# Output projection: the last two pairs of weight tiles taken chunk by chunk, and the norm's steps reordered to match

## The reference, cut to what matters

```
mix = jnp.concatenate([o.reshape(B, S, D_ATTN), rg], axis=-1) @ p['w_out'][l]
x = x + g2 * mix
h = _rmsnorm(x, ng[2]) * (1.0 + sc3) + sh3
x = x + g3 * 0.5 * _swiglu(h, p['ffn_w_gate'][l, 1], p['ffn_w_up'][l, 1], p['ffn_w_down'][l, 1])
```

## Time and profile before

| what | value |
|---|---|
| median of 3 runs | 2269.17 us |
| lowest, highest | 2267.47 us, 2271.68 us |
| time of the profiled execution | 2273.28 us |
| its span in the trace | 2271.5 us |
| PE busy in the span | 97% |
| DVE busy | 68% |
| ACT busy | 36% |
| output projection, pairs 1 to 3 on PE | about 1388.9 to 1465.3 us of the span |

### The profile page before, as it was taken

How to read it: one execution, slowest core, us unless ns; L and a number is a source line. 1 busy time by engine, 2 the same in 40 slices (tenths; PEclk the granted TensorE clock), 3 DMA queues, 4 the chain that set the end, 5 groups by cost and what they waited for, 6 DMA issues and landing times.

```text
span 2271.5 us, 33980 instructions
## 1 busy us (share of the span) xinstructions
PE 2196.6 (97%) x13144; PEld 2108.2 (93%) x13144; DVE 1552.8 (68%) x2607; ACT 816.1 (36%) x1458; POOL 20.2 (1%) x31
## 2 busy tenths in 40 slices
PE   5999999999999999999999999999999999999997
PEld 4989999999999999889977779899999999999996
DVE  6977677777888776666668874686455556756556
ACT  5632322334111143654255662453232323421122
POOL 0000000000000000000000030000000000000000
PEclk8999999999999999999989999999999999999998
DMA  7333333344524304010110011131212123431312
GB/s 290 132 105 133 104 124 113 107 135 134 202 93 158 126 21 156 19 47 29 32 49 22 22 40 38 56 114 60 86 58 87 58 87 101 157 122 52 107 43 84
DMA packets 82292, 210.10 MB, mean 92 GB/s; under 512 B 9856, under 2 KB 36352, under 8 KB 82176
## 3 DMA queue, kind: packets, MB, share of 16 engines
q1 hardware_dynamic: 82176, 208.52, 27.3%
HBM read 172.56 MB, written 35.92 MB: 92 GB/s over the span
## 4 chain that ended last, share of the span: by engine, by line
PE 89%; DVE 6%; DMA 2%; ACT 2%; issue 1%; SPq 1%; DVEq 0%; ACTq 0%
PE ps L717 15%; PE ps L718 15%; PE ps L719 15%; PE ps L792 9%; PE ps L794 9%; PE ps L793 9%; PE ps L972 6%; PE ps L1043 4%; PE ps L1072 2%; PE ps L1058 1%; PE ps L954 1%; DVE sb_nmx L2280 1%; DMA sb_stage<-in_w_mod 1%; DVE sb_hL L1752 1%; PE ps L741 1%
## 5 line engine op out<-in xcount | busy, mean ns | idle before, releaser
L717 PE MATMUL ps<-sb_hH,sb_wH 128*128 128x384 f32 x1664 | 563.1, 338 | 6.3 <-DVE sb_hL L1752 3.4
L718 PE MATMUL ps<-sb_hL,sb_wH 128*128 128x384 f32 x1664 | 557.8, 335 | 0.0
L719 PE MATMUL ps<-sb_hH,sb_wL 128*128 128x384 f32 x1664 | 557.6, 335 | 0.0
L717 PEld LDWEIGHTS ps<-sb_hH,sb_wH 128*128 128x128 f32 x1664 | 313.7, 189 | 13.1 <-DVE sb_hL L1752 4.6
L718 PEld LDWEIGHTS ps<-sb_hL,sb_wH 128*128 128x128 f32 x1664 | 313.7, 189 | 1.2 <-issue 0.3
L719 PEld LDWEIGHTS ps<-sb_hH,sb_wL 128*128 128x128 f32 x1664 | 313.8, 189 | 0.0
L2056 DVE SCALAR_TENSOR_TENSOR sb_x<-ps,sb_mod,sb_x 128x384 f32<-128x384 f32 (+2 forms) x384 | 186.3, 514 | 172.4 <-PE ps L719 167.0
L792 PE MATMUL ps<-sb_hH,sb_wH 128*128 128x384 f32 x704 | 235.4, 334 | 0.5 <-issue 0.3
L794 PE MATMUL ps<-sb_hH,sb_wL 128*128 128x384 f32 x704 | 235.2, 334 | 0.0
L793 PE MATMUL ps<-sb_hL,sb_wH 128*128 128x384 f32 x704 | 235.1, 334 | 0.0
L1226 ACT ACTIVATE sb_wH<-sb_wide 128x512 fp32r<-128x512 f32 x176 | 110.9, 632 | 228.0 <-DVE sb_wide L1806 222.9
(11 more groups left out here) (244 smaller groups left out, 3795.7 us busy)
## 6 DMA issues: line engine op xcount, KB each, us to landing
sb_raw<-in_w_gate SPq DMA_DIRECT2D x56, 512.0 KB, 3.6
sb_raw<-in_w_up SPq DMA_DIRECT2D x56, 512.0 KB, 3.6
sb_raw<-in_w_mod SPq DMA_DIRECT2D x56, 512.0 KB, 3.5
hidden<-sb_tmp SPq DMA_DIRECT2D x132, 192.0 KB, 2.2
sb_hid_raw<-hidden SPq DMA_DIRECT2D x40, 576.0 KB, 6.3
sb_raw<-in_w_dn SPq DMA_DIRECT2D x80, 256.0 KB, 2.6
sb_stage<-in_w_mod SPq DMA_DIRECT2D x4, 2048.0 KB, 15.7
sb_raw<-in_w_in SPq DMA_DIRECT2D x16, 512.0 KB, 3.5
```

The costliest lines, as they stand in the source:

```text
L717: pe.matmul(o, wH, xH, start=begin, stop=False)
L718: pe.matmul(o, wH, xL, start=False, stop=False)
L719: return pe.matmul(o, wL, xH, start=False, stop=end)
```

## The change

Pairs 0 and 1 stay as they are. The weights of pair 3 now go to `wjH` and `wjL`, so that pairs 2 and 3 are resident together, and PE takes these two pairs chunk by chunk: (2,0), (3,0), (2,1), (3,1), (2,2), (3,2). The helper `mix_nth` gives the place of a (pair, chunk, f) in the new order for the semaphore waits. `stats` and `spread` of chunks 0 and 1 move to new places in that order. The running sums of the norm move from `last_raw` to `o_first`. The orders of ACT and DVE are written anew: the `lo` of pair 3 now stands ahead of the nine sums, and the adds of pairs 2 and 3 follow chunk by chunk. The loops over `i` are written out.

```diff
-SQUARES[2] = [(c, k) for ks in (range(4), (4, 5), (6, 7)) for c in range(NC) for k in ks]
+SQUARES[2] = [(c, k) for ks in (range(4), range(4, KT)) for c in range(NC) for k in ks]
...
         def sum_buf(z, c):
 
+            if z == 2:
+                return o_first[:, c * CH:(c + 1) * CH]
             return tmp[:, 4] if z % 2 else last_raw[:, c * CH:(c + 1) * CH]
+
+        def mix_nth(i, c, f):
+
+            return i * 6 + 2 * c + f + 1 if i < 2 else 12 + 4 * c + 2 * (i - 2) + f + 1
...
             def out_chunk(i, c, between=None):
 
+                mH, mL = (wjH, wjL) if i == 3 else (wiH, wiL)
                 for f in range(2):
                     pe.wait_ge(raw_used[f], i + (used_wo[f] + 2))
-                    pe.wait_ge(w_x, i * 6 + (c * 2 + f + 1))
+                    if i:
+                        pe.wait_ge(w_x, 6 + mix_nth(i - 1, c, f))
                     for n, k in enumerate(MIX_ORDER):
-                        if isinstance(i, int) and i == 0:
+                        if i == 0:
                             pe.wait_ge(mix_lo, c * KT + n + 1)
-                        m = three(ps[:, f * NC + c, 0:CH], wiH[:, f, k * P:(k + 1) * P], wiL[:, f, k * P:(k + 1) * P],
+                        m = three(ps[:, f * NC + c, 0:CH], mH[:, f, k * P:(k + 1) * P], mL[:, f, k * P:(k + 1) * P],
...
-            with pe.Fori(0, 2) as i:
-                for c in range(NC):
-                    out_chunk(i + 1, c)
-            def last_chunks(at_stats, at_spread, c, before=None):
+            for c in range(NC):
+                out_chunk(1, c)
+            norm_at = {(2, 1, 8): (stats, 0), (3, 1, 2): (spread, 0), (2, 2, 8): (stats, 1), (3, 2, 8): (spread, 1)}
...
-            out_chunk(3, 0)
-            out_chunk(3, 1, last_chunks(12, None, 0))
-            out_chunk(3, 2, last_chunks(8, 3, 1, 0))
+            for c in range(NC):
+                for i in (2, 3):
+                    out_chunk(i, c, norm_steps(i, c))
             ffn_pe(1)
...
-            with act.Fori(0, 2) as i:
+            for i in range(2):
                 for f in range(2):
-                    cast(wiH[:, f], f, i + (used_wo[f] + 1), (w_ready, i * 6 + (5 + f)))
+                    cast(wiH[:, f], f, i + (used_wo[f] + 1), (w_ready, mix_nth(i, NC - 1, f)))
+            for f in range(2):
+                cast(wjH[:, f], f, 2 + (used_wo[f] + 1))
...
             load_root()
             for c in range(NC):
                 squares(2, c, x_mixed, range(4))
-            for f in range(2):
-                cast(wiH[:, f], f, 2 + (used_wo[f] + 1), (w_ready, 12 + (5 + f)))
+            squares(2, 0, x_mixed, (4, 5))
...
-            with dve.Fori(0, 2) as i:
-                w_adds(i)
+            for f in range(2):
+                lo(wjL[:, f], f, None, wjH[:, f], whi_wo + 7 + f)
             for c in range(NC):
                 for k in range(1, 4):
                     sum_square(2, c, k)
-            w_adds(2)
+            w_add(2, 0, 0)
+            w_add(2, 0, 1)
+            sum_square(2, 0, 4)
+            sum_square(2, 0, 5)
             early_low(1, 0, 0)
             early_low(1, 1, 0)
+            w_add(3, 0, 0)
+            sum_square(2, 0, 6)
             shift_step(1)
-            for c in range(NC):
-                for k in (4, 5):
-                    sum_square(2, c, k)
-            for f in range(2):
-                w_add(3, 0, f)
-            sum_square(2, 0, 6)
+            w_add(3, 0, 1)
             sum_square(2, 0, 7)
-            w_add(3, 1, 0)
+            w_add(2, 1, 0)
+            inverse_of(2, 0)
             early_low(1, 0, 1)
             early_low(1, 1, 1)
-            inverse_of(2, 0)
-            w_add(3, 1, 1)
-            sum_square(2, 1, 6)
-            sum_square(2, 1, 7)
+            w_add(2, 1, 1)
+            sum_square(2, 1, 4)
+            sum_square(2, 1, 5)
...
             def rest(k):
-                if k == 2:
-                    w_add(3, 2, 0)
+                if k == 1:
+                    w_add(3, 1, 0)
+                    sum_square(2, 1, 6)
                 elif k == 3:
-                    inverse_of(2, 1)
+                    w_add(3, 1, 1)
+                    sum_square(2, 1, 7)
                 elif k == 5:
-                    w_add(3, 2, 1)
-                elif k == 7:
-                    sum_square(2, 2, 6)
-                    sum_square(2, 2, 7)
+                    w_add(2, 2, 0)
+                    sum_square(2, 2, 4)
 
             apply(2, 0, rest)
+            inverse_of(2, 1)
+            w_add(2, 2, 1)
+            sum_square(2, 2, 5)
+            for k in (6, 7):
+                w_add(3, 2, k - 6)
+                sum_square(2, 2, k)
             inverse_of(2, 2)
             ffn_dve(1)
```

More of the change, by code:

```diff
@@ L1132, in _, with norm_steps @@
                 out_chunk(0, c, lambda n: outputs(*later[c, n]) if (c, n) in later else None)
-            with pe.Fori(0, 2) as i:
-                for c in range(NC):
-                    out_chunk(i + 1, c)
-            def last_chunks(at_stats, at_spread, c, before=None):
+            for c in range(NC):
+                out_chunk(1, c)
+            norm_at = {(2, 1, 8): (stats, 0), (3, 1, 2): (spread, 0), (2, 2, 8): (stats, 1), (3, 2, 8): (spread, 1)}
+            def norm_steps(i, c):
                 def between(n):
[L1138 to L1143, removed]
-                return between
-            out_chunk(3, 0)
-            out_chunk(3, 1, last_chunks(12, None, 0))
-            out_chunk(3, 2, last_chunks(8, 3, 1, 0))
+                    if (i, c, n) in norm_at:
+                        do, at = norm_at[i, c, n]
+                        do(2, at)
+                return between
+            for c in range(NC):
+                for i in (2, 3):
+                    out_chunk(i, c, norm_steps(i, c))
             ffn_pe(1)
@@ L1617, in _ @@
                     mix_high(c, k)
-            with act.Fori(0, 2) as i:
+            for i in range(2):
                 for f in range(2):
-                    cast(wiH[:, f], f, i + (used_wo[f] + 1), (w_ready, i * 6 + (5 + f)))
+                    cast(wiH[:, f], f, i + (used_wo[f] + 1), (w_ready, mix_nth(i, NC - 1, f)))
+            for f in range(2):
+                cast(wjH[:, f], f, 2 + (used_wo[f] + 1))
             def x_mixed(c, k):
-                return w_x, 6 + (12 if k < 4 else 18) + (2 * c + k - 5 if k > 5 else 0)
+                return w_x, 6 + mix_nth(k // 2, c, k % 2)
             load_root()
@@ L1632, in _ @@
             early_cast(1, 1, 0)
-            for c in range(NC):
-                squares(2, c, x_mixed, (4, 5))
             squares(2, 0, x_mixed, (6, 7))
+            root_of(2, 0)
             early_cast(1, 0, 1)
             early_cast(1, 1, 1)
-            root_of(2, 0)
-            squares(2, 1, x_mixed, (6,))
+            squares(2, 1, x_mixed, (4, 5))
             root_copy(2, 0)
-            squares(2, 1, x_mixed, (7,))
             for k in range(KT):
                 h_hi(2, 0, (k,))
-                if k == 2:
-                    squares(2, 2, x_mixed, (6,))
+                if k == 1:
+                    squares(2, 1, x_mixed, (6,))
                 elif k == 3:
+                    squares(2, 1, x_mixed, (7,))
+                elif k == 5:
                     root_of(2, 1)
-                elif k == 5:
-                    squares(2, 2, x_mixed, (7,))
+                    squares(2, 2, x_mixed, (4,))
+            squares(2, 2, x_mixed, (5,))
             root_copy(2, 1)
+            squares(2, 2, x_mixed, (6, 7))
             root_of(2, 2)
@@ L2355, in w_add @@
             def w_add(i, c, f):
-                dve.wait_ge(w_ready, i * 6 + (2 * c + f + 1))
+                dve.wait_ge(w_ready, mix_nth(i, c, f))
                 for cond, b, e in conds(c):
@@ L2364, in _ @@
             dve.wait_ge(xback, 16 * KT)
-            def w_adds(i):
+            for i in range(2):
                 for c in range(NC):
```

## The result

The changed kernel takes 2275.74 us (median of 10 runs, 2274.62 to 2278.00), the kernel before 2269.64 us (10 runs, 2267.47 to 2274.52). The ratio is 1.0028, with a 95% interval of 1.0019 to 1.0036: slower by 6.1 us, 4.3 to 8.2. The prediction was +5.9 us, 2275.1 us.

What follows compares the result with a forecast made beforehand. PE, busy 97% of the span, was taken to bound the kernel. A stop of +9.5 us, +2.4 for the slow clock and −5.96 at the FFN's start gave +5.9 on 2269.17: 2275.1 us, range 2270.9 to 2279.5.

Steps and rivals of the forecast that it cites:

- What the change can win: At the FFN's start: PE's waits, slow clock and restarts there would go, at most 5.96 us.
- The stop at (3,0): Before pair 3's first matmul on chunk 0: PE waits for `w_add(2, 0, 0)`, 9.5 us, bounds 9.2 to 10.0.
- The clock after it: After the stop at (3,0): PE restarts at a granted clock of 0.50, losing 2.4 us, bounds 1.7 to 2.8.
- The rival with a full clock: After the stop at (3,0): clock does not fall, +3.5 us, 2272.7 us; chance 0.15, shared with the shorter stop.
- The sum: Whole kernel: +9.5 for the stop, +2.4 for the clock, −5.96 at the FFN's start, together +5.9 us.
- The margins behind it: From the restart to the FFN: no further stop; 1.1 us spare at `w_add(2, 2, 1)`, 2.1 at the second spread.
- The rival with a second stop: At `w_add(2, 2, 1)` or the second spread: DVE late, PE stops again, +8.5 us, 2277.7 us; chance 0.14.
- The shorter stop: At (3,0): nine sums at 0.48 us each, 4.3 us not 8.5, giving +1.7 us, 2270.9; chance 0.15, shared with full clock.

Runs made afterwards that it cites:

- The kernel with no wait in the stretch: Changed kernel with DVE's and ACT's queues put in PE's order, each chunk's squares and sums whole in turn; 2263.07 us.
- The two experiments that move one part each: Each against the changed kernel: adds of (2,0) put ahead of the nine sums, 2269.54 us; pair 3's weight tiles loaded early into free buffers, 2271.13 us.
- the 52 useless matmuls: Changed kernel with 52 matmuls of unused result on PE ahead of its wait at (3,0); 2272.71 us.
- the spread late: Kernel before with `spread(2, 1)` moved from the projection's end behind the sixth tile of the FFN's first product; 2270.53 us.
- the adds first: Changed kernel with the adds of (2,0) ahead of the nine sums on DVE; 2269.54 us.

## Why the prediction was right, step by step

*What the change can win.* I had taken 5.96 us from the trace of before, the waits, the clock and the restarts together. The kernel with no wait in the stretch is 5.92 us shorter there. In the changed kernel itself these waits went as forecast, and no new one came at the end.

*The stop at (3,0).* Forecast 9.5 us, bounds 9.2 to 10.0; measured 9.61 from start to start. Its parts stood up too: 6.05 us later for the first sum (forecast 6.1), 8.50 from there to the add. The two experiments that move one part each give the load 3.6 us and show that the add's place in the queue makes the whole stop.

*The clock after it.* Forecast 2.4 us between 1.7 and 2.8; measured 2.78, at the upper bound. This is the one term that was off by more than a tenth or two, and the moment at which the clock rises again, which no row of before could tell, decides it: 2.8, 2.2, 2.1 and 1.6 us after stops of 9.45, 14.11, 5.85 and 3.91 us. That the row of the 5.00 us stop gave the same 2.8 us is as much chance as rule. The Trainium skill (TensorE: Matmul & The Clock Gate, "What's actually happening") has the number of slow matmuls vary from run to run. Each kernel here was profiled once, so no trace shows that for this stop; three kernels with unlike stops have 18, 15 and 14 slow steps, and the last section has one place with the same instructions where the slow time differed from execution to execution. The rival with a full clock, +3.5 us, would have needed PE busy in the stop; with the 52 useless matmuls the kernel comes to +3.94 us in the stretch.

*The sum.* 9.61 + 2.78 − 5.96 = 6.43 us, where the stretch shows 6.56. The remaining 0.13 us are not explained by a row that I read.

*The margins behind it.* The tightest, `w_add(2, 2, 1)`, was forecast at 1.1 us. PE did not wait for it, nor for the second spread, but the margins were smaller than forecast. The timeline of DVE has the add, that of PE the first matmul that wants its bank:

```profile
1468.26 0.61 DVE L2367 SCALAR_TENSOR_TENSOR sb_x<-ps,sb_mod,sb_x 128x384 f32<-128x384 f32 x1
```

```profile
1469.50 0.33 PE L723 MATMUL ps<-sb_hH,sb_wjH 128*128 128x384 f32 x1
```

That leaves 0.6 us, and the second spread had 1.7 us where the forecast had 2.1. The queue is about half a microsecond from a second stop. (The prediction's list of PE's times there starts 0.15 us too early: 1431.5 + 2.4 + 4.16 is 1438.06 and not 1437.9.) The rival with a second stop did not happen here. It did happen, at another place, once the adds alone were moved: taking a late step out of a queue shows the next one.

*The shorter stop.* Squares and sums kept their pace of before, with 0.65 us of handover at each pair, so the rival with sums that run closer together had nothing to it. Its price was also too low: six sums back to back start 3.56 us before the next instruction in the kernel before (1446.73 to 1450.29), 0.59 us each and not 0.48, so nine would take 5.3 us and that rival would come to about 2271.9 us, still 3.8 below the measured time.

## What to carry to other kernels

When a matrix engine's order is changed so that a bank comes back sooner, list what stands ahead of the instruction that frees it on its own engine, loads and casts included, and add up to the time at which it is wanted. PE's new order cost 6 us here while the vector engine's queue kept the sums ahead of the add; with DVE's and ACT's queues in the same order the kernel was 6 us faster than before. Price a stop with the clock after it: 1.6 to 2.8 us came on top of each stop of 2 to 14 us, except where other matmuls filled it.

## What the runs showed of the hardware that I had not expected

**Much of the difference ahead of the stretch comes after one wait.** All nine profiled kernels have the same instructions on PE up to the projection's first matmul, yet this starts at 1352.6 to 1358.8 us of the span. Near 1150 us PE waits 2.4 us for ACT. The granted clock after it (us, PE busy, clock, DMA share, GB/s), in the trace of before, then in that of the changed kernel:

```profile
1150.00:1160.00 10.00, 9.00 (x25) 0.51 0.13 52
1160.00:1170.00 10.00, 9.80 (x52) 0.81 0.01 2
```

```profile
1150.00:1160.00 10.00, 8.84 (x35) 0.83 0.11 45
1160.00:1170.00 10.00, 10.00 (x72) 1.00 0.01 2
```

The kernel before stayed at the lower level for some 13 us there, the changed one for less than 4, after a wait of the same length. From the restart after this wait to the projection's first matmul it is 207.89 us in the one (1150.19 to 1358.08) and 204.05 us in the other (1149.90 to 1353.95). Over all nine profiles it is 204.05 to 207.89 us, 3.8 us of spread; up to 2.5 us more arise before the wait. The three longest, 207.76 to 207.89 us, are the three whose clock stayed below 1.00 past 1160 us. The two go together; no kernel here changes this wait, so that the clock is the cause is not shown by an experiment. The stretch after that point repeats to 0.02 us between two kernels with the same waits.

**Short waits in a row can drop the clock as one longer wait does.** With the spread late, three waits of 1.90, 0.74 and 0.99 us with three matmuls between each two left the granted clock at 0.50. A single wait of 1.60 us in the kernel before left it at 1.00; its timeline of PE, and the stretch with the clock:

```profile
1543.48 0.41 PE L792 MATMUL ps<-sb_r2H,sb_wH 128*128 128x384 f32 x1 [1.60 <-issue]
```

```profile
1542.00:1544.00 2.00, 0.52 (x3) 1.00 0.00 0
```

**The clock can fall after the wait is over.** With the adds first it was at 1.00 through a wait of 3.91 us and fell more than 1 us behind the restart. So a first matmul at full pace does not tell that a stop was free.
